# Last block's up projections: every second tile joined, its half sums copied by ScalarE

## What is computed

```python
f = rms_norm(h, ffn_norm_g[l]) @ w_up[l]           # 256 x 1024 @ 1024 x 5632
f = depthwise_conv(f, ffn_dw_w[l], ffn_dw_b[l])    # 3 taps over the tokens
fg, fu = jnp.split(f, 2, axis=-1)
h = h + (jax.nn.silu(fg) * fu) @ w_down[l]         # 256 x 2816 @ 2816 x 1024
```

## Time and profile before

| | us |
|---|---|
| median of 3 runs | 1285.37 (1284.87 to 1286.46) |
| profiled execution | 1285.6 |
| its span, first to last instruction | 1283.4 |

### The profile page before, as it was taken

One profiled execution on the slowest core, in us unless ns is written; L12 is line 12 of the kernel. 1 busy time (PEld: TensorE's weight loads), 2 busy tenths in 40 slices (PEclk: granted clock), 3 DMA queues, 4 the chain that ended last, 5 costly groups with the idle time before them and its releaser, 6 DMA issues.

```text
span 1283.4 us, 20758 instructions
## 1 busy us (share of the span) xinstructions
PE 1251.5 (98%) x7312; PEld 1056.5 (82%) x7312; DVE 612.8 (48%) x1165; ACT 707.0 (55%) x1091; POOL 715.0 (56%) x335
## 2 busy tenths in 40 slices
PE   5999999999999999999999999999999999999998
PEld 1688668787888888888767658899989977999998
DVE  3424672237444444201066364677743585666621
ACT  3482356336554444422268454777675667877753
POOL 0452234353544444444535034699998874988897
PEclk8999999999999999999999999999999999999999
DMA  9523753742333233633624334565666540655564
GB/s 363 207 98 100 279 198 132 284 163 78 99 101 110 99 98 98 243 102 114 230 96 135 128 128 164 195 202 203 197 208 203 181 138 31 224 197 196 195 206 127
DMA packets 60129, 210.10 MB, mean 164 GB/s; under 512 B 6432, under 2 KB 9760, under 8 KB 59936
## 3 DMA queue, kind: packets, MB, share of 16 engines
q1 hardware_dynamic: 59632, 207.52, 46.9%
q10 hardware_dynamic: 432, 1.70, 0.3%
HBM read 208.15 MB, written 1.05 MB: 163 GB/s over the span
## 4 chain that ended last, share of the span: by engine, by line
PE 72%; POOL 11%; issue 7%; DVE 4%; ACT 3%; DMA 2%; SPq 1%; POOLq 0%; DVEq 0%; ACTq 0%
PE ps L387 51%; POOL wlo L374 11%; PE ps L407 3%; PE ps L545 2%; DMA raw<-wstream 2%; PE ps L408 1%; PE ps L1688 1%; PE ps L1667 1%; PE ps L1266 1%; PE ps L1254 1%; PE ps L464 1%; ACT whi L369 1%; SPq L347 1%; PE ps L446 1%; PE ps L456 1%
## 5 line engine op out<-in xcount | busy, mean ns | idle before, releaser
L374 POOL TENSOR_TENSOR wlo<-raw,whi 128x1024 fp32r<-128x1024 f32 x291 | 687.0, 2381 | 493.9 <-ACT whi L369 493.7
L369 ACT ACTIVATE whi<-raw 128x1024 fp32r<-128x1024 f32 x291 | 306.8, 1058 | 190.0 <-PE ps L387 94.7
L387 PE MATMUL ps<-Hlo_,whi 128*128 128x256 f32 (+1 forms) x1440 | 293.3, 309 | 0.1
L387 PEld LDWEIGHTS ps<-Hlo_,whi 128*128 128x128 f32 x1440 | 200.9, 191 | 15.2 <-issue 3.2
L387 PE MATMUL ps<-Hhi_,whi 128*128 128x512 f32 (+1 forms) x528 | 180.5, 365 | 0.0
L861 ACT ACTIVATE u<-ps,par 128x256 f32<-128x256 f32 (+1 forms) x132 | 82.7, 627 | 72.4 <-PE ps L387 67.6
L407 PE MATMUL ps<-hid,whi 128*128 128x512 f32 x352 | 115.9, 383 | 0.9 <-DVE hid L937 0.9
L387 PE MATMUL ps<-Hhi_,wlo 128*128 128x512 f32 (+1 forms) x488 | 111.1, 370 | 0.0
L407 PE MATMUL ps<-Hhi_,whi 128*128 128x512 f32 x336 | 110.2, 382 | 0.0
L387 PEld LDWEIGHTS ps<-Hhi_,whi 128*128 128x128 f32 x528 | 94.0, 189 | 14.1 <-issue 2.4
L920 DVE SCALAR_TENSOR_TENSOR u<-ps,par,u 128x255 f32<-128x255 f32 (+1 forms) x132 | 72.9, 552 | 65.7 <-ACT u L861 65.6
(11 more groups left out here) (371 smaller groups left out, 2080.4 us busy)
## 6 DMA issues: line engine op xcount, KB each, us to landing
raw<-wstream SPq DMA_DIRECT2D x367, 512.0 KB, 3.5
Haside_lo<-wstream SPq DMA_DIRECT2D x8, 512.0 KB, 6.1
Haside_hi<-wstream SPq DMA_DIRECT2D x8, 512.0 KB, 9.1
Paside<-wstream SPq DMA_DIRECT2D x4, 512.0 KB, 5.2
XT<-x_t SPq DMA_DIRECT2D x1, 1024.0 KB, 10.1
XT<-ctx_t SPq DMA_DIRECT2D x1, 1024.0 KB, 12.3
memx<-mem_t ACTq DMA_DIRECT2D x1, 1024.0 KB, 5.6
out_t<-XT SPq DMA_DIRECT2D x1, 640.0 KB, 6.5
```

The source lines that it names most:

```text
L369: nc.scalar.activation(whi[:, n % RING, :], raw[:, r % RAWS, :], ACT.Copy).then_inc(S["hi_ready"], 1)
L374: nc.gpsimd.tensor_tensor(wlo[:, r, :], raw[:, r, :], whi[:, n % RING, :].bitcast(F32), ALU.subtract).then_inc(S["lo_ready"], 1)
L387: mm = nc.tensor.matmul(o, a, b, start=start, stop=stop)
```

## The change

Of the last block's up tiles, the odd ones from tile 3 on are joined instead of split (21 of 44; tile 1 belongs to first_tiles and stays). For each of them ScalarE copies the half sum in columns 256 to 511 to half_sums, ahead of the Identity of that tile, as soon as TensorE has finished it; VectorE then adds it to the other half in PSUM and multiplies by 1/rms as before, which waits for the add. VectorE's wait for the tile becomes a wait for the copy. f_r counts two per tile now. The semaphore m_kpc is renamed part_copied, keeps its one increment, and counts the copies from there on.

```diff
--- before.py
+++ after.py
@@ -171,7 +171,7 @@
         for t in ("f0", "f1", "f2"):
             names += f" {t}_u {t}_c1 {t}_free {t}_s {t}_hf {t}_hi {t}_pair {t}_dn"
         names += " z1 gqk gvc g_z g_abs g_l g_zd g_G g_b g_e g_q g_kt g_kst g_sc g_am g_decay g_U g_S g_o g_of g_ot g_oc g_sr g_vec g_yh g_y go_x"
-        names += " m_dn m_csq m_css m_cstd m_chi m_cn m_clo m_half m_kpc m_ev m_qsq m_qss m_qlog m_qrstd m_qn m_ksq m_kss m_klog m_krstd m_kn m_sw m_rot"
+        names += " m_dn m_csq m_css m_cstd m_chi m_cn m_clo m_half part_copied m_ev m_qsq m_qss m_qlog m_qrstd m_qn m_ksq m_kss m_klog m_krstd m_kn m_sw m_rot"
         names += " a_s a_max a_exp a_pn a_t a_pt a_o a_oh mo_x"
         names += " t_tab t_sin t_gsw e_sq e_tot e_ss e_rv e_xn e_hi e_lo"
         names += " s_vm s_gg s_pad s_cv s_sq s_ev s_ss s_rr s_xg s_sw s_nrm s_vc s_mu s_xc s_csq s_cvs s_crstd s_cn s_cs s_chi s_ch"
@@ -802,7 +802,7 @@
             def up_tile(j, i):
 
                 pe.wait_ge(S[f"{t}_free"], i * 8 + j + 1)
-                if f != 1:
+                if f == 0 or f == 2 and j % 2 == 0:
                     column_tile(pe, s0 + j, j % 4, xhi, xlo, ntok, i)
                 else:
                     joined_products(pe, s0 + j, i, j % 4, 0, KD, lambda k: rows[:, k], xhi, True, True)
@@ -852,8 +852,12 @@
 
                 act.wait_ge(S[f"{t}_pair"], i * 4 + q + 1)
                 for j in (2 * q, 2 * q + 1):
+                    joined = f == 2 and j % 2 == 1 and j >= 3
+                    if joined:
+                        act.wait_ge(S["slot_used"], i * 8 + used(s0 + j))
+                        nc.scalar.activation(half_sums(j // 2), ps[:, j % 4, T:TT], ACT.Copy).then_inc(S["part_copied"], 1)
                     if f == 2:
-                        act.wait_ge(S["f_r"], 4 * FF_T - 4 + i * 8 + j + 1)
+                        act.wait_ge(S["f_r"], 4 * FF_T - 4 + 2 * (i * 8 + j + 1))
                     elif f == 1 and j >= 2:
                         act.wait_ge(S["f_r"], 2 * (i * 8 + j - 1))
                     else:
@@ -909,8 +913,14 @@
             def scaled(j, i):
 
                 tile = ps[:, j % 4, 0:T]
-                dve.wait_ge(S["slot_used"], i * 8 + used(s0 + j))
-                nc.vector.tensor_tensor(tile, tile, rstd[:, T:TT], ALU.mult).then_inc(S["f_r"], 1)
+                joined = j % 2 == 1 and j >= 3
+                if joined:
+                    dve.wait_ge(S["part_copied"], 1 + i * 4 + j // 2)
+                    nc.vector.tensor_tensor(tile, tile, half_sums(j // 2), ALU.add).then_inc(S["f_r"], 1)
+                    dve.wait_ge(S["f_r"], 4 * FF_T - 4 + 2 * (i * 8 + j) + 1)
+                else:
+                    dve.wait_ge(S["slot_used"], i * 8 + used(s0 + j))
+                nc.vector.tensor_tensor(tile, tile, rstd[:, T:TT], ALU.mult).then_inc(S["f_r"], 1 if joined else 2)
 
             def taps(q, i):
 
@@ -1638,7 +1648,7 @@
                     nc.tensor.matmul(ps[:, 4 + j % 4, :], ones if j < 4 else blk64, Hf1[:, j, :], start=True, stop=True).then_inc(S["m_qss"], 1)
                 if s == 7:
                     pe.wait_ge(S["late_in"], 16)
-                    pe.wait_ge(S["m_kpc"], 1)
+                    pe.wait_ge(S["part_copied"], 1)
                     pe.wait_ge(S["m_qn"], 5)
                     nc.tensor.matmul(ps[:, 4, 0:T], mlac[:, 0:P], kpe[:, T:TT], start=True, stop=True).then_inc(S["m_sw"], 1)
                     pe.wait_ge(S["m_qn"], 6)
@@ -1774,7 +1784,7 @@
                     down_std(2)
                 if s == 1:
                     act.wait_ge(S["m_cn"], 5)
-                    nc.scalar.activation(kpe[:, :], ps[:, 5, :], ACT.Copy).then_inc(S["m_kpc"], 1)
+                    nc.scalar.activation(kpe[:, :], ps[:, 5, :], ACT.Copy).then_inc(S["part_copied"], 1)
                 if half != 0 and n + RING < START["mo"]:
                     hi_slot(act, n + RING)
                 if s in (2, 4, 5, 6):
@@ -1881,7 +1891,7 @@
             key_split(3, third)
             latent_norm(5)
             query_squares(1)
-            dve.wait_ge(S["m_kpc"], 1)
+            dve.wait_ge(S["part_copied"], 1)
             dve.wait_ge(S["late_in"], 16)
             nc.vector.tensor_tensor(Hf1[:, 7, 0:T], ps[:, 5, T:TT], cos, ALU.mult).then_inc(S["m_rot"], 1)
             dve.wait_ge(S["m_clo"], 4)
```

## The result

| | before | after |
|---|---|---|
| median, in the same comparison (us) | 1285.12 | 1316.22 (1316.04 to 1318.51, 4 runs) |
| ratio, 95% interval | | 1.0246 (1.0234 to 1.0257) |
| profiled execution (us) | 1285.6 | 1316.09 |
| its span (us) | 1283.4 | 1313.9 |

The change makes the kernel 31.1 us slower, 2.5%. The forecast was 1314 with a range of 1306 to 1322.

A forecast was written before the change was run, and what follows sets the result against it. TensorE bounded the last block's up projections before; afterwards a ScalarE-VectorE series of 6.69 us a pair against 5.30 would. TensorE's restart 28.5 us later, added to 1285.6, gave 1314.1, forecast as 1314 us; range 1306 to 1322.

The forecast's parts named there:

- TensorE's gain: Last block's up projections: a joined tile takes 2.62 us instead of 2.68, saving 1.3 us at most over 21 tiles.
- The ring: Up projections: each copy waits for the previous pair to pass through ScalarE and VectorE, 6.69 us against TensorE's 5.30.
- Both bounds above: Up projections: add to scaling up to 0.62 us, hi_slot to copy up to 1.12; together +6.6 us, giving 1321.
- Start and end of the stretch: Up projections: second copy at 1122.07, last copy at 1249.7, TensorE resuming the down projections at 1256.0, 28.5 us later.
- The 22 slots behind it take what they took.: Down projections after TensorE resumes with the third slot: their duration stays as in the kernel before.
- The third rival: Up projections: TensorE's clock falls to 0.50 through 1.4 us gaps a pair, 105 us longer, 1390 us; chance 0.02.
- part 4 of the prediction: End of the up projections: last scaling to TensorE's third down slot takes 5.41 us; restart at 1256.0; 1314 us forecast.
- Its sign: From 1110 us on the profile's time line, where the up projections run: TensorE's granted clock under 1.
- TensorE stays the bound: Up projections: copy and scaling slip into idle gaps, only the 1.3 us saving of joined tiles remains, 1284 us; chance 0.07.
- The delay is paid once: Up projections: Silu and hi copy catch up within each pair, leaving one lag at the end, about 1287 us; chance 0.04.
- Load of ScalarE: Up projections, posed with the experiments: engines' work sums decide, so ScalarE's idle 1.1 us a pair absorbs extra work, 1316 us.

The follow-up runs named there:

- second copy: Changed kernel with another ScalarE copy of the same 256 columns, to an unused place, just ahead of the first; 1322.21 us.
- split with the copy: Changed kernel with all tiles split into 24 products, ScalarE's copy (now columns 0 to 255) and VectorE's add kept, result wrong; 1318.92 us.
- copy before hi_slot: Changed kernel with ScalarE's copy of the odd tile moved up between the even tile's Identity and its hi_slot; 1295.21 us.

## Why the prediction was right, point by point

- **TensorE's gain.** Joined tiles at 2.62 us: pairs at 5.30 us with them alone, and the stage 1.2 us shorter where 1.3 was given as the most. (The medians differ by 1.9 and the spans by 1.6, but 0.3 of that lies ahead of the stage.) Right, and without weight, as was said.
- **The ring.** Right in every link to 0.06 us: 0.95, 0.41, 0.47, 3.01, 1.90 measured; 0.95, 0.43, 0.46, 3.01, 1.84 taken. The sum was 0.05 short. The term that was mis-sized is Silu to hi_slot: VectorE's product starts 0.49 behind Silu (1159.23 to 1159.72), where it was 0.43 in the earlier trace rows. Nineteen rings times 0.05 is nearly all of the 1.0 us by which the stretch was underestimated (29.5 against 28.5). Both bounds above (add to scaling 0.62, hi_slot to copy 1.12) were not needed.
- **Start and end of the stretch.** The first ring was 6.31 us (6.29 taken), the last copy at 1250.05 (1249.7), and TensorE restarted at 1256.33 (1256.0):

```profile
1115.09 0.39 ACT L858 ACTIVATE modrow<-ps 128x256 f32<-128x256 f32 x1
...
1121.40 0.37 ACT L858 ACTIVATE rstd<-ps 128x256 f32<-128x256 f32 x1
```

```profile
1250.05 0.39 ACT L858 ACTIVATE modrow<-ps 128x256 f32<-128x256 f32 x1
```

  That the last two agree to 0.35 us is in part luck: the stage began 0.7 us earlier than in the profile of before, and the stretch was 1.0 us longer than worked out.

- **"The 22 slots behind it take what they took."** Wrong by 1.65 us. The first two down slots were done early, as stated, so TensorE stood still for 4.53 us instead of 0.21, and its clock fell. The third rival had the mechanism, weighed it against the gap of 1.4 us a pair, where it did not occur, and overlooked the one long gap at the end that part 4 of the prediction itself describes. Its sign, a clock under 1 behind 1110, did show, but for some 3 us and not for the stretch.
- **The total.** For the profiled execution 1314.1 was worked out and 1316.09 measured: 1.0 from the ring, 1.65 from the clock and -0.7 from the start of the stage. The range held the result, but its upper bound was made of two links that stayed as they were; nothing in it stood for the clock.
- **The rivals.** TensorE stays the bound: refuted for the kernel after, and true for the copy by VectorE, since there the series is shorter than 5.30. The delay is paid once: refuted, each pair has the same 6.74. Load of ScalarE: refuted by the second copy.

The Trainium skill, "Perfetto Trace Analysis", section "Optimizing Scalar/DVE Operations", says that work may be moved to ScalarE where VectorE is saturated. VectorE was busy for 71 of 113 us here, not saturated by its sum, and the move is what costs: with the copy on VectorE 1284.7, with it on ScalarE 1316.2. The rule looks at load, and no row contradicts it as far as that goes; what decided was the place in the queue.

## What to carry to other kernels

When a step is handed to another engine, walk once around all the engines' queues from that step to its next turn and add the start-to-start distances; if the sum is over the period of the engine that sets the pace, every turn pays the difference, whatever idle time the busy shares show. Place such a step ahead of the long instructions that nobody waits for soon (here hi_slot, four tiles early), or leave it on the engine that needs the result. And when the pacing engine gets ahead of a stage's end, ask what its standing still does to its clock.

## What the runs showed of the hardware

- TensorE's granted clock fell to 0.50 behind gaps of 4.53 us (kernel after and its repetition), 4.55 (split with the copy) and 4.80 (second copy), for 3 us or more. That made the down projections longer by 1.65, 2.48, 2.98 and 2.40 us; two executions of the same kernel differ in it by 0.8. It stayed at 1.00 behind 2.64 us (copy before hi_slot) and through gaps of 1.2 us in each pair. With the gap filled it stayed at 1.00.
- A plain float32 product of 256 columns stands in the profile as two and takes 0.427 us, an fp32r one 0.112.
- ScalarE's copies of 256 columns from PSUM start 0.27 us apart though each is recorded with 0.38.
